# TensorE takes the steps of attention in pairs, in a stick-breaking attention layer on one core

## What is computed

```python
proj = jnp.einsum('bsd,de->bse', rmsnorm(x, a_norm), w_in)
q, k, v, g = jnp.split(proj, 4, axis=-1)
z = jnp.einsum('bthd,bshd->bhts', q, k) * scale          # per head
log_rem = jnp.where(s_idx < t_idx, jax.nn.log_sigmoid(-z), 0.0)
after = lax.cumsum(log_rem, axis=3, reverse=True) - log_rem
w = jnp.where(s_idx < t_idx, jnp.exp(jax.nn.log_sigmoid(z) + after), 0.0)
o = jnp.einsum('bhts,bshd->bthd', w, v)
x = x + jnp.einsum('bse,ed->bsd', o * jax.nn.silu(g), w_out)
out = rmsnorm(x, final_norm)
```

## Time and profile before

| | |
|---|---|
| median of three runs | 1704.89 us (1700.06 to 1705.18) |
| profiled execution | 1704.25 us, span from first to last instruction 1702.5 |
| TensorE matmul busy | 1655.9 us, 97% |
| VectorE busy | 1312.2 us, 77% |
| ScalarE busy | 878.1 us, 52% |
| granted clock, mean | 0.997 |

### The profile page before, as it was taken

The page is one execution under the profiler, slowest core; times in us unless marked ns, Lnnn a source line. Parts: engine busy times, 40 slices in busy tenths (PEclk is TensorE's granted clock), DMA queues, the critical chain, the costliest instruction groups (busy, mean ns, idle before and its releaser), DMA issues.

```text
span 1702.5 us, 23181 instructions
## 1 busy us (share of the span) xinstructions
PE 1655.9 (97%) x8600; PEld 1376.5 (81%) x8600; DVE 1312.2 (77%) x1855; ACT 878.1 (52%) x1749; POOL 256.8 (15%) x220
## 2 busy tenths in 40 slices
PE   5999999999999999999999999999999999889998
PEld 4778878888888888888888888888888888768886
DVE  5530058888898989888888888898888898986763
ACT  5431135656555556555565656565556556652121
POOL 0010012011110121101110111012201111306600
PEclk9999999999999999999999999999999999999999
DMA  6842243334334242424333333344252426469732
GB/s 247 254 124 50 63 143 112 103 119 113 118 106 124 72 152 69 137 64 148 92 113 99 112 106 114 98 118 121 78 135 79 141 59 216 131 195 316 240 120 78
DMA packets 157025, 216.11 MB, mean 127 GB/s; under 512 B 49136, under 2 KB 90096, under 8 KB 156912
## 3 DMA queue, kind: packets, MB, share of 16 engines
q1 hardware_dynamic: 87424, 139.05, 26.2%
q10 hardware_dynamic: 69488, 75.58, 14.8%
HBM read 139.01 MB, written 75.56 MB: 126 GB/s over the span
## 4 chain that ended last, share of the span: by engine, by line
PE 81%; DVE 7%; DMA 5%; issue 2%; ACT 2%; POOL 1%; SPq 1%; ACTq 1%; DVEq 0%
PE proj_ps L679 26%; PE turn_ps L706 12%; PE proj_ps L637 7%; PE o_ps L720 7%; PE z_ps L696 7%; PE z_ps L697 7%; PE o_ps L721 7%; PE turn_ps L747 4%; PE z_ps L747 3%; PE proj_ps L747 3%; DVE u L1064 2%; DMA x_rows<-in_x 2%; POOL w_raw L607 1%; DVE r_turned_lo L1069 1%; PE o_ps L747 1%
## 5 line engine op out<-in xcount | busy, mean ns | idle before, releaser
L849 ACT ACTIVATE u<-z_ps 128x512 f32<-128x512 f32 (+3 forms) x640 | 341.0, 533 | 421.0 <-PE z_ps L697 416.3
L1064 DVE TENSOR_TENSOR_SCAN u<-u,u 128x512 f32<-128x512 f32 x384 | 497.7, 1296 | 0.0
L1069 DVE TENSOR_TENSOR r_turned_lo<-turn_ps,r_turned_hi 128x512 fp32r<-128x512 f32 (+3 forms) x640 | 376.8, 589 | 39.9 <-ACT r_turned_hi L855 38.6
L855 ACT ACTIVATE r_turned_hi<-turn_ps 128x512 fp32r<-128x512 f32 (+3 forms) x640 | 340.0, 531 | 64.1 <-issue 45.9
L607 POOL TENSOR_SCALAR w_raw<-w_raw,a_norm_col 128x128 f32<-128x128 f32 x192 | 176.8, 938 | 1202.6 <-DMA w_raw<-in_w_qkg 1202.6
L706 PE MATMUL turn_ps<-ident,u 128*128 128x128 f32 x2176 | 343.6, 273 | 0.0
L679 PE MATMUL proj_ps<-hT_hi,w_hi 128*128 128x512 f32 x768 | 319.9, 417 | 0.0
L679 PE MATMUL proj_ps<-hT_hi,w_lo 128*128 128x512 f32 x768 | 319.6, 416 | 0.0
L679 PE MATMUL proj_ps<-hT_lo,w_hi 128*128 128x512 f32 x768 | 319.5, 416 | 0.0
L706 PEld LDWEIGHTS turn_ps<-ident,u 128*128 128x128 f32 x2176 | 268.3, 140 | 59.7 <-issue 0.4
L720 PE MATMUL o_ps<-r_turned_hi,dv_head 128*128 128x512 f32 (+3 forms) x640 | 233.2, 364 | 14.5 <-DVE r_turned_lo L1069 13.5
(11 more groups left out here) (105 smaller groups left out, 1678.1 us busy)
## 6 DMA issues: line engine op xcount, KB each, us to landing
qk_hi_cols<-made_hi ACTq DMA_DIRECT2D x64, 256.0 KB, 2.5
qk_lo_cols<-made_lo ACTq DMA_DIRECT2D x64, 256.0 KB, 3.0
w_raw<-in_w_qkg SPq DMA_DIRECT2D x24, 512.0 KB, 3.5
x_rows<-in_x SPq DMA_DIRECT2D x16, 512.0 KB, 5.7
x_T<-in_xT SPq DMA_DIRECT2D x16, 512.0 KB, 4.5
v_rows<-v_stage ACTq DMA_DIRECT2D x32, 256.0 KB
v_here<-v_rows SPq DMA_DIRECT2D x64, 128.0 KB, 2.8
v_next<-v_rows SPq DMA_DIRECT2D x64, 128.0 KB, 3.0
```

The costliest lines, as they stand in the source:

```text
L849: nc.scalar.activation(u_t[(m // CB) % RU][STEPS[m][3]][:, 0:w], z_ps[m % RZ][:, 0:w], ACT.Sigmoid, scale=-Z_SCALE).then_inc(s_u, 1)
L855: nc.scalar.activation(rt_hi[m % RT][:, 0:w], t_ps[m % RT][:, 0:w], ACT.Copy).then_inc(s_hi, 1)
L1064: nc.vector.tensor_tensor_scan(u, u, other, start, ALU.mult, op).then_inc(s_r, 1)
L1069: nc.vector.tensor_tensor(rt_lo[m % RT][:, 0:w], t_ps[m % RT][:, 0:w], as_f32(rt_hi[m % RT][:, 0:w]), ALU.subtract).then_inc(s_lo, 1)
```

## The change

TensorE's loop takes two steps at a time, n even: scores of steps n + 9 and n + 10, turns of steps n + 2 and n + 3, the projections of both, and then the weighings of steps n and n + 1. The loops of the other engines stay as they are. The SBUF buffers of turned tiles become four (`RR`), on two free places; for one of these the second output stage is given up (`RO` is 1). The banks `turn_ps` stay three, so a turn now waits itself for the low part of the step three before, where before the weighing's wait stood for that.

```diff
-RU, RZ, RT, RO, RP = 3, 2, 3, 2, 2
+RU, RZ, RT, RR, RO, RP = 3, 2, 3, 4, 1, 2
...
                     pe.wait_ge(s_r, m - m % CB + CB)
+                    if m >= RT:
+                        pe.wait_ge(s_lo, m - RT + 1)
...
-                    nc.tensor.matmul(o_ps[:, 0:w], weights, rt_hi[m % RT][:, 0:w], start=begin, stop=False)
-                    last = nc.tensor.matmul(o_ps[:, 0:w], weights, rt_lo[m % RT][:, 0:w], start=False, stop=end)
+                    nc.tensor.matmul(o_ps[:, 0:w], weights, rt_hi[m % RR][:, 0:w], start=begin, stop=False)
+                    last = nc.tensor.matmul(o_ps[:, 0:w], weights, rt_lo[m % RR][:, 0:w], start=False, stop=end)
...
-                for n in range(-LEAD_SCORES, NS):
-                    if inside(n + LEAD_SCORES):
-                        scores(n + LEAD_SCORES)
-                    if inside(n + LEAD_TURN):
-                        if n + LEAD_TURN == RT - 1:
-                            pe.wait_ge(s_vT, 1)
-                        turn(n + LEAD_TURN)
-                    project(filled(n - 1), filled(n))
-                    put_out(out_filled(n - 1), out_filled(n))
-                    if inside(n):
-                        weigh(n)
+                for n in range(-LEAD_SCORES - 1, NS, 2):
+                    pair = (n, n + 1)
+                    for m in pair:
+                        if inside(m + LEAD_SCORES):
+                            scores(m + LEAD_SCORES)
+                    for m in pair:
+                        if inside(m + LEAD_TURN):
+                            if m + LEAD_TURN == RT - 1:
+                                pe.wait_ge(s_vT, 1)
+                            turn(m + LEAD_TURN)
+                    project(filled(n - 1), filled(n + 1))
+                    put_out(out_filled(n - 1), out_filled(n + 1))
+                    for m in pair:
+                        if inside(m):
+                            weigh(m)
```

More of the change, by code:

```diff
@@ L40 @@
 AT_U = BASE + 32 * KB
-AT_RT = BASE + 56 * KB
+AT_RT = [(BASE + 56 * KB + 4 * KB * n, BASE + 58 * KB + 4 * KB * n) for n in range(3)] + [(BASE + 82 * KB, BASE + 92 * KB)]
 AT_DV = BASE + 68 * KB
@@ L144, in filled @@
 def filled(n):
-    made = BEFORE * QPM + LEAD_FILL * min(n + 1 + LEAD_SCORES, LEAD_SCORES)
+    made = BEFORE * QPM + LEAD_FILL * max(0, min(n + 1 + LEAD_SCORES, LEAD_SCORES))
     return min(made + max(n + 1, 0) * FILL_NUM // FILL_DEN, NG * QPM)
@@ L284, in all_stages @@
         u_t = [[place(nc, f"u{n}_{r}", [P, CH], F32, AT_U + 2 * KB * (CB * n + r)) for r in range(CB)] for n in range(RU)]
-        rt_hi = [place(nc, f"r_turned_hi{n}", [P, CH], F32R, AT_RT + 4 * KB * n) for n in range(RT)]
-        rt_lo = [place(nc, f"r_turned_lo{n}", [P, CH], F32R, AT_RT + 4 * KB * n + 2 * KB) for n in range(RT)]
+        rt_hi = [place(nc, f"r_turned_hi{n}", [P, CH], F32R, at[0]) for n, at in enumerate(AT_RT)]
+        rt_lo = [place(nc, f"r_turned_lo{n}", [P, CH], F32R, at[1]) for n, at in enumerate(AT_RT)]
         o_st = [place(nc, f"o_stage{n}", [P, CH], F32, AT_OST + 2 * KB * n) for n in range(RO)]
@@ L554, in _ @@
                         sp.wait_ge(s_gst, stores_through(GROUP_OF["g", KT - 1, 0]))
-                        for par in range(2):
-                            sp.wait_ge(s_oout[par], 32 * (H - 2) * NC // 2)
+                        for par in range(RO):
+                            sp.wait_ge(s_oout[par], 32 * (H - 2) * NC // RO)
                         load_group(0, slice(0, KT - 1), s_in[0])
@@ L854, in hi @@
                     act.wait_ge(s_t, m + 1)
-                    nc.scalar.activation(rt_hi[m % RT][:, 0:w], t_ps[m % RT][:, 0:w], ACT.Copy).then_inc(s_hi, 1)
+                    nc.scalar.activation(rt_hi[m % RR][:, 0:w], t_ps[m % RT][:, 0:w], ACT.Copy).then_inc(s_hi, 1)
                 def empty(e):
@@ L1068, in lo @@
                     dve.wait_ge(s_hi, m + 1)
-                    nc.vector.tensor_tensor(rt_lo[m % RT][:, 0:w], t_ps[m % RT][:, 0:w],
-                                            as_f32(rt_hi[m % RT][:, 0:w]), ALU.subtract).then_inc(s_lo, 1)
+                    nc.vector.tensor_tensor(rt_lo[m % RR][:, 0:w], t_ps[m % RT][:, 0:w],
+                                            as_f32(rt_hi[m % RR][:, 0:w]), ALU.subtract).then_inc(s_lo, 1)
                 def piece_sum(i):
```

## The result

| | before | with the change |
|---|---|---|
| median of six runs each, same chip | 1704.22 us (1700.06 to 1705.27) | 1717.93 us (1714.31 to 1720.7) |
| profiled execution, span | 1704.25, 1702.5 us | 1714.31, 1712.6 us |

The ratio is 1.0078 (95% interval 1.0067 to 1.009): 13 us slower, where 1722 had been forecast.

The account below looks back on a forecast made before the run. The prediction took the length of TensorE's queue to bound the kernel, with VectorE close behind. It summed 1704.25 - 1.3 (borders) - 2 (old waits) + 21 (new waits) to 1722 us, 1% slower, range 1697 to 1735.

Parts of the forecast that it names:

- Fewer changes of kind: TensorE's queue: 320 fewer cycles of borders between kinds of instruction, 1.3 us of gain, with 0 and 10.6 as ends.
- nothing is left for a border: TensorE, three turns to the second projection: 0.56 us equals 3 x 0.11 + 0.23, so borders cost nothing there.
- My fit: TensorE's cycles between 260 and 1440 us, summed with a projection's price free: 0.004 us a cycle left unexplained.
- The turn of the odd step, and the projections behind both turns: TensorE waits for VectorE's low part behind groups ending in even steps: 35 of 42 short, 21 us; 2 us taken off.
- Odd ends: Projection groups ending in an odd step: weighing of step n+3 as far from the group's end as before, cost nothing.
- Second scores: The pair's second scores need the sigmoid of two steps back; ScalarE is early, so cost nothing.
- One output stage: ScalarE's copy of a finished chunk must wait for the previous store: cost nothing, 16 us at the very worst.
- SyncE's queue: Load of q for a head gets some 7 us against 3.4 needed: cost nothing, else up to 1 us per head.
- The end: Behind step 618, with no projections and VectorE already late: left as it is in the sum.
- The loop of 10 to 14 us: Rival at the end: pairs tie late VectorE to TensorE, 10 to 14 us on top, 1734 us; chance 0.10.
- No drains: Rival: turns between matmuls drain TensorE like a tiling-mode change; fewer drains would give 1621 us; chance 0.01.
- Borders cost the whole and the waits stay small: Rival, every TensorE cycle: borders cost all 0.033 us, gain 10.6 us, new waits under 5, 1697 us; chance 0.16.

Follow-up runs that it names:

- experiment 5: The changed kernel with the second turn moved behind the first step's projections, scores and weighings still in pairs: 1707.29 us, ratio 1.0004 to the kernel before.
- experiment 1: The changed kernel with ScalarE and VectorE taking projection groups that end in an even step one iteration later: 1704.28 us, ratio 0.9989 to the kernel before.
- experiment 3: The changed kernel with low parts of groups ending in even steps, and the stores behind them, held back on VectorE alone: 1703.66 us, ratio 0.9987.
- Experiment 12: The kernel of experiment 1 with ScalarE taking both sigmoids of a pair before the first turn's high part: 1701.08 us, ratio 0.9974 to the kernel before.
- experiment 4: The kernel before with one output stage in place of two and nothing else: 1705.21 us, ratio 0.9998.
- experiment 9: The kernel of experiment 1 with the first step's projections moved ahead of both turns: 1708.97 us, ratio 1.0017 to the kernel before.
- experiment 10: The kernel of experiment 1 with pairs only in steps 10 to 549 and single steps around them: 1700.24 us, ratio 0.9963 to the kernel before.
- experiment 7: The changed kernel with both steps' projections moved ahead of both turns: 1768.6 us, ratio 1.0362 to the kernel before.

## Why the prediction was right, and where not

The forecast of 1722 us was 4 us high; its mechanism is what happened. In the profiled executions its sum of +17.7 us came out at +10.1, or +13.4 without the 3.3 us by which the untouched V stage happened to be shorter. That it came so close is in part luck. The new waits before turns are 13.1 us where I had 21, the old ones before weighings gave back 5.9 (7.1 to 1.2 by the starts) where I took off 2, and the borders gained 5.9 where I took 1.3. Against these 16.4 us too high stand terms that I had at nothing: second scores (5.9 us of waits and 3.7 of small delays), the start (1.3) and the end (2.6).

*Fewer changes of kind.* This term was mis-sized: I took 1.3 us of gain, and the middle alone gave 5.9, inside my ends of 0 and 10.6. The step that failed is the sentence "nothing is left for a border". I looked for the price at the border, at two decimals, and there the stretch is the plain sum of its parts even in experiment 5, which pays. About 0.013 us of the price is at the border of a group of turns (0.006 before it, 0.007 behind), too little for two decimals, and the rest is in the run behind it. So the steps of 0.23 and 0.24 within a run, which I held against a price of borders, are that price. My fit gave the same 0.004 for the same reason: it let the projections' price float, and with seven products beside every two groups of turns the one could take up the other (argued, not tested). My test, spacing inside a run, would have misled as well. I had written that 0.227 would give borders away; with the change the mean is 0.230, before 0.231.

*The turn of the odd step, and the projections behind both turns.* Right in mechanism, and nearly so in size at the place that was worked out: low part of step 96 at 3.30 us behind the last product of step 94 in both traces. I had 0.30 us of standstill behind that; by the starts it is 0.46. The sum leaves out the 0.146 us from the low part's end to the waiting turn's start; that the row says 0.30 as well is chance, since it counts from the modelled end of the turn before. Over all groups I had 21 us in 35 places, and measured 13.1 us in 36 late turns, with 16.3 us of waiting of every kind behind even ends, in 32 pairs over 0.05 us late. So nearly all the places were right and the sum 8 us too high, although 0.146 us was missing from each. Experiments 1 and 3 show that it is VectorE's queue. I had counted each group by itself and let no wait shorten the next, so the sum had to be an upper one; how much of the 8 us that explains wasn't measured. My sign, a row "turn_ps <- DVE r_turned_lo" of 12 to 25 us, shows only 6.8 us under that name; the rest of it stands in PEld's rows under other names.

*Odd ends* were costed at nothing: 5.1 us now, 3.3 with the even ends held. Nearly right.

*Second scores.* This term was missing: costed at nothing, and 4.1 and 3.7 us of waits for sigmoids appeared in TensorE's two lines, where before there was none; by the starts they are 5.9 us. The cover I named, ScalarE's early sigmoids, is thinner than its 391.7 us of idle time made it look: it is at 277.9 now, and at places with extra pieces in its queue it is gone. Experiment 12 shows that it can be closed; by the two ratios that is worth 0.15%, which their intervals don't set apart from nothing.

*One output stage:* nothing in the kernel before, as experiment 4 shows. *SyncE's queue:* no wait for a q load in the changed kernel, one of 0.9 to 1.9 us in experiments 1, 3, 9 and 12.

*The end.* Left as it was; it lost 2.6 us from step 579 on. The loop of 10 to 14 us isn't there. Experiment 10 loses 1.4 us there without pairs, which would leave 1.2 us to the pairs. The waits from 1440 to 1560 us, to hold against the earlier trace rows:

```profile
ACT o_stage L867 <- DMA o_lo_cols<-o_stage: 7.0, 2, 4.9
...
PE turn_ps L708 <- DVE r_turned_lo L1075: 8.8, 6, 2.4
...
PE o_ps L722 <- DVE r_turned_lo L1075: 3.4, 7, 1.0
```

TensorE's waits for VectorE are 12.2 us where they were 10.8; they moved from weighings to turns. ScalarE's wait for its one stage, which I had costed at nothing, shows here for once, at most within those 2.6 us.

*The start* gained 2.0 us, but 3.3 had been gained at the end of the V stage, in code that is the same; the pairs cost 1.3 us there, which I hadn't in the sum.

*The rivals.* No drains: the Trainium skill, TensorEngine Tiling (Array Packing), Key Properties, has TensorE drain when its tiling mode changes, and experiment 5 measures that a border of turns with products doesn't act like one: a drain would bare 0.16 us at each, and a whole pair saves 0.05 at most. "Borders cost the whole and the waits stay small" failed by its waits, not by its borders, of which half were there; experiment 1 brings its small waits about but gains only 0.1%, and experiment 10, at 0.9963 of the kernel before, comes near its 1697 of 1704.

## What to carry to other kernels

When several engines follow orders written by hand, an edit of one order moves its instructions against all the others: find the instruction behind which another engine's queue stands idle (here a group's low part, at 41 places), and work out at such a place who needs what is queued behind it. Having found it, change the other engine's order with the edit, one line here: 0.8% slower became 0.4% faster once VectorE's queue was shifted and the pairs kept to the middle. And price a small effect over a whole repeat of the pattern with everything in it fixed, not at the spot where you think it sits. When you compare two profiled executions, look first at a stretch that the edit doesn't touch: here it differed by 3.3 us, a third of what was to be explained.

## What the runs showed of the hardware

Behind 128x128 fp32 turns, float32r matmuls start further apart: 0.224 to 0.236 us for up to ten matmuls of 512 columns, where the same matmuls ahead of the turns, or in a long run, start 0.2267 apart. Each border adds little, 0.006 us before the first turn and 0.007 behind the last. Over a full pair, two groups make 4.33 to 4.35 us; one makes 4.29 in most pairs of the change, but 4.33 in a third of them and 4.31 to 4.32 in experiment 9, where only three or four products follow the turns. All of this is from starts in the traces; the cause is open.

An instruction that TensorE holds back for VectorE starts 0.146 us behind the end of what it waits for, at all 36 late turns.

Idle time tells little of slack. ScalarE is busy 52% of the span, and moving turns by seven products against its queue (experiment 7) still cost 62 us against the kernel before and some 48 against the change (1.0362 over 1.0078), of which putting the sigmoids first in its queue gave back 34.
